# Half-width level and late-block matrices in the two blocked triangular inverses of a one-core transformer kernel

## The reference, cut to what matters

```python
a_mat = beta[..., :, None] * jnp.einsum('nhcid,nhcjd->nhcij', k, k) * d_strict
rhs = jnp.concatenate([beta[..., None] * v, (beta * gam)[..., None] * k], axis=-1)
sol = lax.linalg.triangular_solve(a_mat, rhs, left_side=True, lower=True, unit_diagonal=True)
```

```python
def step(s, inp):
    r_t, w_t, k_t, v_t, kk_t, b_t = inp
    sa = jnp.einsum('nhij,nhj->nhi', s, -kk_t)
    s = s * w_t[:, :, None, :] + sa[..., None] * b_t[:, :, None, :] + v_t[..., None] * k_t[:, :, None, :]
    y = jnp.einsum('nhij,nhj->nhi', s, r_t)
    return s, y
```

## Time and profile before

| | |
|---|---|
| runs of the kernel, us | 1298.08, 1298.20, 1293.09; median 1298.08 |
| profiled execution, its own time | 1295.21 us |
| its span in the profile | 1293.3 us |
| mean granted TensorE clock | 0.992 of full speed |
| instructions | 18494 |

### The profile page before, as it was taken

One profiled execution on the slowest core, in us unless ns is written; L12 is line 12 of the kernel. 1 busy time (PEld: TensorE's weight loads), 2 busy tenths in 40 slices (PEclk: granted clock), 3 DMA queues, 4 the chain that ended last, 5 costly groups with the idle time before them and its releaser, 6 DMA issues. The chain is left out here.

```text
span 1293.3 us, 18494 instructions
## 1 busy us (share of the span) xinstructions
PE 1229.6 (95%) x7285; PEld 878.4 (68%) x7285; DVE 749.8 (58%) x1467; ACT 345.8 (27%) x748; POOL 51.9 (4%) x92
## 2 busy tenths in 40 slices
PE   6999999999999999999999999999899999998997
PEld 5877549995447674699844478657566686575683
DVE  3254466775352145676743549875884378848872
ACT  2253312120012144121100222333441232434422
POOL 1100000000000000000000000200300000203000
PEclk9999999999999999999999999999999999999999
DMA  9731105454553431354544433310010632300000
GB/s 297 255 121 66 65 15 209 168 181 150 190 186 125 145 130 66 131 194 137 192 176 151 177 116 129 130 67 2 1 51 1 205 139 80 131 2 1 2 2 33
DMA packets 65853, 149.25 MB, mean 115 GB/s; under 512 B 2097, under 2 KB 8135, under 8 KB 65767
## 3 DMA queue, kind: packets, MB, share of 16 engines
q1 hardware_dynamic: 62432, 141.63, 31.0%
q0 software_dynamic: 1216, 3.52, 1.0%
q10 hardware_dynamic: 2119, 2.91, 0.9%
HBM read 146.95 MB, written 1.07 MB: 114 GB/s over the span
## 5 line engine op out<-in xcount | busy, mean ns | idle before, releaser
L1366 ACT ACTIVATE region<-banks 128x384 f32<-128x384 f32 (+8 forms) x159 | 77.0, 484 | 304.1 <-PE banks L442 105.0
L442 PE MATMUL banks<-hnT,weight_slabs 128*128 128x256 f32 x576 | 126.6, 380 | 3.4 <-DVE hnT L1841 3.4
L442 PEld LDWEIGHTS banks<-hnT,weight_slabs 128*128 128x128 f32 x576 | 108.8, 190 | 20.1 <-DVE hnT L1841 4.1
L494 PE MATMUL banks<-weight_slabs,region 128*128 128x512 f32 x256 | 115.1, 592 | 0.0
L494 PEld LDWEIGHTS banks<-weight_slabs,region 128*128 128x128 f32 x256 | 48.5, 190 | 60.3 <-issue 60.3
L494 PE MATMUL banks<-region 128*128 128x512 f32 x192 | 87.6, 592 | 0.0
L1824 DVE TENSOR_TENSOR region<-weight_slabs 128x1024 f32<-128x1024 f32 x32 | 39.2, 1225 | 80.3 <-PE banks L494 76.4
L1824 DVE TENSOR_TENSOR region<-region 128x256 f32<-128x256 f32 (+23 forms) x160 | 75.7, 473 | 17.1 <-ACT region L1711 12.0
L1982 DVE TENSOR_TENSOR region<-banks,region 128x128 f32<-128x128 f32 x40 | 11.7, 292 | 117.8 <-PE banks L609 91.2
L1824 DVE TENSOR_TENSOR region<-weight_slabs,region 128x1024 f32<-128x1024 f32 x64 | 78.2, 1221 | 1.1
L1322 POOL TENSOR_TENSOR region<-region,consts 128x240 f32<-128x240 f32 (+24 forms) x60 | 34.4, 599 | 957.1 <-DVEq L1833 934.2
(11 more groups left out here) (363 smaller groups left out, 2050.7 us busy)
## 6 DMA issues: line engine op xcount, KB each, us to landing
weight_slabs<-in_mlp_w SPq DMA_DIRECT2D x32, 2048.0 KB, 8.7
weight_slabs<-in_w_in SPq DMA_DIRECT2D x10, 2048.0 KB, 7.8
weight_slabs<-in_od_w_in SPq DMA_DIRECT2D x6, 2048.0 KB, 8.1
weight_slabs<-in_ev_w_in SPq DMA_DIRECT2D x4, 2048.0 KB, 11.1
weight_slabs<-in_w_out SPq DMA_DIRECT2D x4, 2048.0 KB, 8.4
weight_slabs<-in_ev_w_out SPq DMA_DIRECT2D x2, 2048.0 KB, 8.0
weight_slabs<-in_od_w_out SPq DMA_DIRECT2D x2, 2048.0 KB, 7.7
weight_slabs<-in_w_in SPq DMA_DIRECT2D x2, 2016.0 KB, 7.5
```

The lines of the kernel that those rows point to most:

```text
L442: ins = mm(view(ps, b + i * S, (1, S)), view(slabs, o + k * width + c0, (1, P)), view(hnT, k * S, (1, S)), start=k == 0, stop=k == KC - 1)
L494: ins = mm(view(ps, b, (1, 512)), view(R, act + k * st, (1, P)), view(w, wt + k * step_, (1, 512)), start=n == 0 and k == 0, stop=n == 7 a ...
L1366: say(A(dst, view(ps, b, *(dims or ((1, n),)), np_=np_), ACT.Copy, scale=scale), read("scalar", *key))
```

## The change

- The level matrix and the late blocks are held in 64 columns for each system, not 128. A mask operation of VectorE thus covers 512 elements in a partition for "r" and 768 for "g", where it covered 1024 and 1536. There are two level matrices and two late-block matrices for each call, so four such operations in each of the four calls.
- So that the multiply stays one instruction, the two 64x64 squares on the diagonal must stand in the same columns. ScalarE does this: a new `matrix_halves` makes two copies, one for each half of the partitions, of all systems' squares into `W.MH`. Its two events are new: VectorE raises `matrix_ready` at the start of `invert`, ScalarE raises `matrix_halves_ready`, and `level_matrix` waits for that.
- `level_matrix(0)` moves from before the 15 base steps to behind step k = 12.
- The masks in the constants and the operand addresses of L840 and L853 follow. TensorE's instructions are the same in number, size and order. SP's and GpSimd's queues are unchanged.

```diff
-            c[:, C_MQ[n]:C_MQ[n] + P] = (j // m == i // m) & np.where(early, j >= i, j <= i)
-            c[:, C_ML[n]:C_ML[n] + P] = (j // (2 * m) == i // (2 * m)) & (j // m != i // m)
+            own = 64 * (j // 64) + np.arange(64)[None, :]
+            c[:, C_MQ[n]:C_MQ[n] + 64] = (j // m == own // m) & np.where(early, j >= own, j <= own)
+            c[:, C_ML[n]:C_ML[n] + 64] = (j // (2 * m) == own // (2 * m)) & (j // m != own // m)
...
-        self.M, self.LT, self.ST, self.XT = (GM, GLT, P, XTG) if g else (RM4, RM4 + 4096, 512, XTR)
+        self.M, self.ST, self.XT = (GM, P, XTG) if g else (RM4, 512, XTR)
+        self.LT, self.MH, self.LS = (GLT, GLT + 768, 64) if g else (RM4 + 4096, RM4 + 4096 + 64, 512)
...
-   ... view(R, W.LT + sy * W.ST + q, (1, 64), p0=q, np_=64),
+   ... view(R, W.LT + sy * W.LS, (1, 64), p0=q, np_=64),
-   ... view(R, W.QT + sy * P + q, (1, 64), p0=q, np_=64),
+   ... view(R, W.QT + sy * 64, (1, 64), p0=q, np_=64),
...
+            def matrix_halves(tag, st):
+                W = PAIRS[st]
+                act.wait_ge(*at("matrix_ready", tag, 0))
+                for q in (0, 64):
+                    ins = A(view(R, W.MH, (W.LS, W.NS), (1, 64), p0=q, np_=64), view(R, W.M + q, (W.ST, W.NS), (1, 64), p0=q, np_=64), ACT.Copy)
+                    if q == 0:
+                        step(ins)
+                    else:
+                        say(ins, up("matrix_halves_ready", tag, 0))
...
                 say(A(view(R, GP, (1, 1536)), view(R, GC, (1, 1536)), ACT.Square), up("gdn_squares_ready", L))
+                matrix_halves(("r", L), "r")
                 copy_out(view(R, LOW + 376, (1, 376)), "low", L, 1, n=376)
...
                 say(A(view(hn, QN + 576 + 64, (672, 2), (1, 32)), view(R, LOW + 344, (376, 2), (1, 32)), ACT.Copy), up("uprojected", L))
+                matrix_halves(("g", L), "g")
                 gate_tanh(0, 0)
...
                 def level_matrix(n):
-                    say(V.tensor_tensor(view(R, W.LT, (W.ST, NS), (1, P)), view(R, W.M, (W.ST, NS), (1, P)),
-                                        view(cst, C_ML[n], (0, NS), (1, P)), MUL), up("level_matrix_ready", tag, n))
+                    dve.wait_ge(*at("matrix_halves_ready", tag, 0))
+                    say(V.tensor_tensor(view(R, W.LT, (W.LS, NS), (1, 64)), view(R, W.MH, (W.LS, NS), (1, 64)),
+                                        view(cst, C_ML[n], (0, NS), (1, 64)), MUL), up("level_matrix_ready", tag, n))
+                signal("matrix_ready", tag, 0)
...
-                level_matrix(0)
...
                     between("base", k)
+                    if k == 12:
+                        level_matrix(0)
...
-                    nb = P // m
+                    nb = 64 // m
-                    say(V.tensor_tensor(view(R, W.QT, (P, NS), (m, nb), (1, m)), vt, view(cst, C_MQ[n], (0, NS), (m, nb), (1, m)), MUL),
+                    say(V.tensor_tensor(view(R, W.QT, (64, NS), (m, nb), (1, m)), vt, view(cst, C_MQ[n], (0, NS), (m, nb), (1, m)), MUL),
                         up("late_blocks_ready", tag, n))
```

More of the change, by code:

```diff
@@ L44 @@
 C_MP = (1228, 1244, 1276)
-C_MQ = (1340, 1468)
-C_ML = (1596, 1724)
+C_MQ = (1340, 1404)
+C_ML = (1468, 1532)
 C_B16 = 1852
@@ L839, in invert @@
                             for q in (0, 64):
-                                ins = mm(view(ps, b + h * m, (1, m), p0=q, np_=64), view(R, W.LT + sy * W.ST + q, (1, 64), p0=q, np_=64),
+                                ins = mm(view(ps, b + h * m, (1, m), p0=q, np_=64), view(R, W.LT + sy * W.LS, (1, 64), p0=q, np_=64),
                                          view(R, W.Pk + sy * m, (1, m), p0=q, np_=64), start=True, stop=True)
@@ L852, in invert @@
                             for q in (0, 64):
-                                ins = mm(view(ps, b + h * m, (1, m), p0=q, np_=64), view(R, W.QT + sy * P + q, (1, 64), p0=q, np_=64),
+                                ins = mm(view(ps, b + h * m, (1, m), p0=q, np_=64), view(R, W.QT + sy * 64, (1, 64), p0=q, np_=64),
                                          view(R, W.Yk + sy * m, (1, m), p0=q, np_=64), start=True, stop=True)
```

## The result

| | before | after |
|---|---|---|
| median of 12 runs, us (lowest, highest) | 1295.54 (1292.13, 1303.38) | 1285.15 (1280.71, 1290.47) |
| ratio, with its 95% interval | | 0.9916 (0.9899 to 0.9933) |
| profiled execution, span, us | 1293.3 | 1288.3 |
| mean granted clock | 0.992 | 0.987 |

The changed kernel is 0.84% faster: 10.9 us of 1295.5 by the ratio, 8.7 to 13.1 by its interval. The forecast was 8.5 us and 1289.6 us. Of the 4.4 us between forecast and time, 2.5 are not the change's: the forecast starts from a median of 1298.08 us of three runs of the kernel before, and the median of twelve is 1295.54.

What follows compares the result with a forecast made beforehand. TensorE was taken as the bound, so VectorE's savings buy only TensorE's waits: 2 x 2.06 ("r") + 2 x 2.2 ("g") = 8.5 us. From a median of 1298.08 us this gave 1289.6 us, range 1283.5 to 1295.5.

Steps and rivals of the forecast that it cites:

- "r": The inverse "r", one call in each of layers 2 and 3: 2.06 us gained a call from base and levels.
- Its base: Base steps of "r": GpSimd's rows come on time and TensorE starts earlier, 0.8 us a call, bounds 0 and 1.2.
- Its levels: Levels of "r": TensorE's waits of 0.26 us at L840 and 0.99 us at L864 go.
- The base of "g": Base steps of "g": step 0 starts 0.7 to 0.8 us earlier, so the L1133 wait ends 0.8 us sooner.
- The levels of "g": Levels of "g": the 0.58 us wait goes but for 0.1, the 0.88 us wait goes; 0.5 + 0.88 us.
- The prices of the half-width masks: VectorE's mask operations: 0.70 us for 512 elements in "r", 0.96 us for 768 in "g".
- The copies at nothing: ScalarE's two copies for the level matrix cost 0, up to 0.5 us a call if a bank is late.
- since that idle stays, so does that: In "g", the clock of 0.61 at 916 to 920, after the 2.85 us of idle, was expected to stay.
- Hidden anyway: Rival, chance 0.08: TensorE is the bound at every place; 0 to 3 us gained, 1295 to 1298 us.
- only the levels: Rival, chance 0.19: base steps do not start TensorE earlier; 4 to 6.5 us gained, 1291.5 to 1294 us.
- Slower: Rival, chance 0.03: base steps collide with GpSimd's picks at the port; up to 5 us lost, 1298 to 1303 us.
- More than forecast: Rival, chance 0.10: less idle spares layer 3's clock fall at 1141 to 1144; 10 to 12 us gained, 1286 to 1288.

Runs made afterwards that it cites:

- copies_twice: The changed kernel with ScalarE's copies made twice, four passes instead of two; 1288.53 us, ratio 0.9916 to the kernel before.
- warm_in_stall: The kernel before with three dummy matmuls on TensorE in its 2.85 us wait at L1133 in "g"; 1294.02 us, ratio 0.9967.
- late_alone: The kernel before with only the late blocks in 64 columns, level matrices full width at their old place, no copies; 1292.65 us, ratio 0.9942.
- block_put_back: The changed kernel with two extra 64-column mask multiplies at the first level matrix's old place; 1295.71 us, ratio 0.9978 to the kernel before.
- again: The changed kernel, unedited, run for a second profile; 1287.27 us, ratio 0.992 to the kernel before.
- change_third: The changed kernel, unedited, on the other chip; 1289.34 us, ratio 0.9929 to the kernel before.
- move_alone: The kernel before with only the first level matrix moved behind base step 12, at full width, no copies; 1294.97 us, ratio 0.9972.
- late_and_move: The kernel before with late blocks in 64 columns and the first level matrix moved at full width, no copies; 1291.26 us, ratio 0.9922.
- change_and_warm: The changed kernel with two dummy matmuls in the L1135 wait of "g" and one at L1051 behind "r"; 1285.68 us, ratio 0.9893.

## Why the prediction was right, and where it was not

**The terms of the sum.** "r" was to give 2.06 us a call and gave 2.20. Its base was the 0.81 us, and the move alone gave 0.92 / 0.85. Its levels were 0.26 + 0.99, and the late blocks alone gave 1.06 / 1.07; both waits are gone. The base of "g" was to give 0.8 us (0.4 to 1.2) and gave 1.18: in the timeline of VectorE the first `tt` starts 1.55 us behind TensorE's first base matmul (914.91 and 913.36), where it was 2.16 (909.23 and 907.07), and takes 0.81 us where it took 1.08. So the earlier start was 0.61 us, less than the 0.7 to 0.8 of the prediction.

```profile
914.35 0.53 DVE L2263 TENSOR_TENSOR region<-banks,region 128x360 f32<-128x360 f32 x1 [1.97 <-PE banks L831]
914.91 0.81 DVE L1839 TENSOR_TENSOR region<-region 128x360 f32<-128x360 f32 x1
```

I had counted only the earlier start. That the steps also become shorter, since GpSimd's picks are further ahead of them, I had set aside as a bound. Up to L1135 it gives 0.75 us: 0.28 at this `tt`, 0.08 at each of the next two, and 0.04 and 0.28 at the first two steps of the rotary embedding (582 and 652 ns before, 540 and 377 after). 0.61 + 0.75 = 1.36 us, and 0.18 come off because the first base matmul itself starts that much later. So this term was the one mis-sized, by 0.38 us a call: it put the earlier start 0.1 to 0.2 us too high, the shorter steps at nothing and the new event at nothing.

The prediction also read a wait wrongly. The 2.0 us at L829 of the earlier trace rows are not the 0.81 us of "r", which the list has apart, but stand in "g", at the second base matmul:

```profile
909.29 0.83 PE L829 MATMUL banks<-region,consts 128*128 128x336 f32 x2 [1.02 <-POOL region L1322]
```

It is the wait for the pick of 2263 ns. It is gone after, but the sum was right not to price it: TensorE would else have waited that much longer at L1133, which ends only when VectorE's chain does. The levels of "g", 0.5 + 0.88 = 1.38, gave 1.42 / 1.58. The prices of the half-width masks were 0.70 and 0.96 us:

```profile
L2295 DVE TENSOR_TENSOR region<-region,consts 128x768 f32<-128x768 f32 x4 | 3.8, 958 | 0.4
L2238 DVE TENSOR_TENSOR region<-region,consts 128x768 f32<-128x768 f32 x4 | 3.8, 958 | 0.5 <-PE banks L842 0.4
...
L2295 DVE TENSOR_TENSOR region<-region,consts 128x512 f32<-128x512 f32 x4 | 2.8, 692 | 0.4
```

They are 0.692 and 0.958. VectorE's busy time fell by 15.3 us, not 12.4. Of the 2.9 us beyond, 1.4 are `tt` steps that lose less to the picks (1086 ns before and 812 after at 360 elements, 571 and 434 at 240, and some 80 ns each at 336 and 312) and 0.6 the two rotary steps; the rest is not followed up. All these terms together were 8.5 us and measured 9.8.

**The copies at nothing.** Nearly right. A copy of 768 elements costs what the nearest row said, 0.84 us, and no wait in the list of TensorE's names them. What the prediction did not cost is the event that orders them, 0.18 us of *g base* on VectorE, inside the bound of 0.5:

```profile
L1578 ACT ACTIVATE region<-region 64x768 f32<-64x768 f32 x4 | 3.4, 844 | 0.1
```

I called it "if barely"; `copies_twice` shows that even twice the copies would cost 0.25 us a call, because the bank that comes late then shortens the wait at L1135 right behind it.

**The step that failed.** It is the sentence on the clock behind the 2.85 us of idle: "since that idle stays, so does that". The idle stayed, at 2.45 us, but the slow clock mostly did not, and 1.69 us a layer came that the sum did not have, up to 3.4 us. The wait was shorter by 0.4 us, and the one of 1.0 us ahead of it, at L829, had gone. `warm_in_stall` shows that the 1.69 us are clock alone. In the profiled executions without dummies, the stretch is slow in 6 of 6 cases with the old start of the base (before, late_alone, block_put_back) and in 3 of 12 with the new (after, again, change_third, move_alone, late_and_move, copies_twice). With dummies it is slow in 0 of 8. These counts show that the slow clock is rarer with the new start of the base. They do not show that the shorter last wait makes it so: `block_put_back` has the change's 2.44 us there, is slow in 2 of 2, and differs by waits of 0.2 to 0.4 us ahead of it, and `copies_twice`, with two waits of 1.4 us, is slow in 0 of 2. What in the idle before it decides was not separated.

**The rivals.** *Hidden anyway* and *only the levels* fell: the waits in the base of "r" and in the levels are gone and gave what they held. *Slower* fell too. Its collisions are there, but they cost less than before and not more: the first `tt`, of 360 elements, takes 0.81 us against 0.56 for a free pass of 384, some 0.25 us too long, where it had been 0.5. *More than forecast* named the size about right, 10 to 12 us, for another reason than the true one. It expected the fall in layer 3 at 1141 to 1144 to go:

```profile
1140.00:1144.00 4.00, 3.76 (x23) 3.79 (x24) 0.00 (x0) 0.77 (x2) 0.00 (x0) 0.69 0.00 0
```

The fall is there again. *between* takes one of three values, 33.5, 35.1 or 38.2 us, in every kernel without dummies there, with the change or not (7, 9 and 4 of the 20 stretches). With the whole change in them the counts are 2, 6 and 2 of 10, without it 5, 3 and 2 of 10; whether the change loads this draw, by up to 0.5 us a layer in these means, such counts can't tell.

**The sum again.** 9.8 us, 0.35 us in *mid* that all kernels with half-width level matrices show, and the clock behind the wait, 3.4 us in three cases of four, some 2.5, make 12.7. Measured were 10.9 (8.7 to 13.1), and by `again` and `change_third` some 10 and 9. What could come off is *start*: it averages 828.6 us in the eight profiled executions with the whole change in them and 825.3 in the other five, though no instruction there differs, and the single values (821.0 to 831.8) overlap. The timed runs speak for the clock here too. Taken to equal clock by the 1.1 us for 0.001 (see `late_alone`), `again` and `change_third` are 9.8 and 9.2 us faster than the kernel before, beside 9.8 + 0.35 in the stretches, and `block_put_back` is 5.5, beside 5.6. So the steps that the change frees are worth some 10 us, and what a set of runs shows above or below that is what clock it drew. By the same estimate `move_alone` has 4.2 us where the stretches have 3.0 and `late_alone` 2.5 where they have 3.8, so it is good to a microsecond or so. Whether the change itself moves the clock outside the inverses stays open.

## What to carry to other kernels

Ask of a long VectorE multiply with two SBUF inputs not only who waits for its result but what it holds up on its own engine and whether GpSimd wants to run at that moment: here the place alone was worth some 0.9 us a call in "r" through GpSimd's rows, and 1.4 in "g" through VectorE's own steps. At full width the multiply did not fit the gap of "g", and 0.7 us of this came back as waits; half the width fitted. Sort a small gain by stretches between the same instructions: those that repeat to 0.02 us carry the change, those that jump between two or three values carry the clock, and one pair of profiles shows 5.0 us where 13.1 went and 8.1 came back. In a wait of 1.5 to 3 us of TensorE that can't be removed, a dummy matmul that ends before the wait does is a cheap thing to try (the change with three such dummies a layer: ratio 0.9893 and 0.9897, the lowest two here, within the interval of the change); one that stands on the path costs more than it saves.

## What the runs showed of the hardware

- The granted clock can fall to 1.2 GHz behind waits as short as 1.46 us, as in the change at L1051 (0.50 in 872 to 874), and even 18 us after the last wait that the timeline shows: in `change_and_warm` that wait, of 0.40 us, ended at 870.22, and behind the 6- and 12-column matmuls above the clock was 0.50. For the same program and the same wait it falls in some executions and not in others (3.94 or 5.35 us behind L1135).

```profile
871.24 3.09 PE L1051 MATMUL banks<-region 128*128 128x64 f32 x16 [1.46 <-ACT region L1608]
```

```profile
872.00:874.00 2.00, 2.00 (x11) 2.00 (x10) 0.00 (x0) 0.39 (x1) 0.00 (x0) 0.50 0.00 0
```

  The Trainium skill ("TensorE: Matmul & The Clock Gate", section "A second HAM failure mode: psum-queue depth-cycling") says of a bf16 kernel that frequent micro-idles between groups of matmuls made its clock swing. The waits of 1.46 to 2.85 us here, with 0.50 and 0.61 behind them, agree that it takes no long idle.
- The block of GpSimd by a two-input multiply of VectorE lasts to the end of each instruction, not of a series: one of 2.40 us held a pick to 2263 ns, two half-width ones let a pick through behind each, after 1465 and 1445 ns. In all three cases the held pick ended 0.6 us behind the multiply. The block works both ways: the multiply that takes 2.40 us beside the picks takes 1.76 in `move_alone`, without them. The Trainium skill ("SBUF — State Buffer", section "SBUF: two separate sides") states this lock for whole instructions; these numbers agree.
- An operation of ScalarE from SBUF to SBUF on 64 partitions takes as long as one on 128: 844 ns for 768 elements, against 0.84 us.
